# Routing spread over the output projection, and the last expert pair summed by TensorE, in a two-layer trunk with a mixture of experts

## The chip, the cores and the metric

One core of a Trainium2 chip runs the whole program. The metric is the device time of one execution in microseconds, the median over runs. All data is float32.

## What is computed

A trunk of two layers over 512 tokens of width 1024. Each layer is a token mixer (RWKV-7 in layer 0, stick-breaking attention in layer 1), a cross-attention into 256 memory rows, and a mixture of experts; each is normed before and added to `h`. The expert part of the reference, cut to what matters:

```python
g_logits = (t @ wg) + bg                       # 4 groups
group = jnp.argmax(g_logits, axis=-1)
p_group = jnp.take_along_axis(softmax(g_logits), group[:, None], axis=-1)
e_sel = ((t @ we) + be).reshape(-1, G, E)[group]   # 8 experts of that group
top_val, top_idx = lax.top_k(e_sel, 2)
top_w = softmax(top_val) * p_group
y = sum over the two experts: top_w * (silu(t @ w1) * (t @ w3)) @ w2
```

So each token goes to 2 of 32 experts. An expert has 3 MB of weights, 96 MB a layer.

## The kernel before

Every engine has its own instruction list, written out by hand, and they meet in semaphores (`S(name)`, `wait_ge`, `then_inc`). `h` lies in SBUF as four tiles of 128 tokens (`NT` = 4). Weights of the projections go through a ring of three 2 MB buffers (`ring`); the arena is shared out by address.

**The projection before the experts** (`cross_pe`, `project_tok`, L548). The output projection `xo` of the cross-attention runs in eight groups of eight matmuls: the four tiles for the left 512 columns, then for the right. DVE adds each to `h` (`add_to_h`, L578). In the right half PE turns the tile before (`late_turn`, L473, half way through a group), ACT and DVE copy the turned parts out (L483, L485), and after the group PE makes that tile's 36 scores (`route_logits`, L1661).

**Routing** (`moe_route_vec`, from L1704). When all four tiles have scores, DVE works out for all of them together: norm scale, best group, first and second expert, a running count (`chosen`). PE ranks the tokens within an expert with a triangular matrix (L1669, L1670). DVE then finds each token's slot, also those beyond 64 rows of an expert (overflow), makes 16 one-hot matrices, and PE sums products of them into a table of which token stands in which slot (L1674). The table is written at L1802. ACT scales the rows of `h` (L1682) and SP stores them to memory (`moe_rows_out`, L1829).

**The experts** (`moe_pe`). There are 16 pairs of experts, 64 rows each, n = 0 to 15. For each POOL gathers 128 rows (L1881), PE turns them (L1935), DVE copies them (L1940), PE multiplies up (L1950), ACT and DVE make the hidden row (L1955 to L1961), PE turns it (L1965) and multiplies down (L1975), ACT and DVE copy the result (L2041, L2061), POOL scatters it to memory (`ye_out`, L1906). PE's order is: up(n), turned hidden of n-1, turned rows of n+1, down(n-1). SP loads the weights (`moe_loads`, L1832, L1833 up, L1836 down). Pair 0's are loaded early, those of pair 1 (into the ring) after the projection, pair 2's up weights into a third buffer `w13x` once `h`'s rows are stored; everything later waits for `up_done` or `down_done` of an earlier pair.

**Overflow and combination.** `further` is a loop over overflow blocks; it reads their number from SBUF and here no block runs. Then POOL gathers for each tile the two rows of every token (`moe_combine_pool`, L1918), when all scatters have landed, and DVE adds both with their gates (`moe_combine_vec`, L1928). SP waits for these gathers, then loads the next layer's `sqkv` weights (L288). In layer 0 PE turns the tiles for the next mixer (L473) and starts its projection `sq` (L534); in layer 1 the final norm follows (`final_vec`, L418, L2179).

## Time and profile before

| what | us |
|---|---|
| median of 3 runs | 1868.31 (1867.97 to 1869.39) |
| the profiled execution | 1867.32 |
| its span | 1865.5 |
| busy PE, DVE, ACT, POOL | 1604.1, 581.8, 412.7, 167.6 |
| DMA moved | 313.84 MB |
| clock of PE over the span | 0.935 of 2.4 GHz |

Times in rows are microseconds from the start of the span. Busy shares mix stages with different limits, so the stages are to be read one by one; a window's row gives the busy time of each engine in it.

### The profile page before, as it was taken

How to read it: one execution, taken by the hardware profiler on the slowest of the kernel's cores; microseconds unless marked ns; L12 is line 12 of the kernel's file. 1: busy time of each engine (PE TensorE's matmuls, PEld its weight loads, DVE VectorE, ACT ScalarE, POOL GpSimd, SP SyncE). 2: the span in 40 equal slices, each digit the busy share in tenths (PEclk: the TensorE clock that was granted, in tenths of full speed). 3: DMA queues.
4: the chain of work that ended last, by engine and by line, in shares of the span. 5: the costliest groups of instructions: out<-in, count | busy, mean ns of one | idle time of the engine just before them, and what ended most of it. 6: DMA issues, size and time to landing. Idle time of an engine off the chain costs nothing.

```text
span 1865.5 us, 26366 instructions
## 1 busy us (share of the span) xinstructions
PE 1604.1 (86%) x11505; PEld 835.6 (45%) x11505; DVE 581.8 (31%) x1040; ACT 412.7 (22%) x805; POOL 167.6 (9%) x186
## 2 busy tenths in 40 slices
PE   4999989998899999669778589999999993988781
PEld 2444468886554454423233244446544542333330
DVE  5210766663651031332111221206310315121114
ACT  2103245553301221201000120017320312010001
POOL 2000123230000000011111200000000000111102
PEclk8999999999899999879899889999999996999896
DMA  6118000000541500279999541220033006799994
GB/s 227 45 58 297 0 3 4 4 4 28 207 150 45 225 1 4 112 295 417 425 423 425 227 172 72 90 77 14 1 136 135 4 0 280 288 423 425 425 397 160
DMA packets 82068, 313.84 MB, mean 168 GB/s; under 512 B 18088, under 2 KB 19168, under 8 KB 57184
## 3 DMA queue, kind: packets, MB, share of 16 engines
q1 hardware_dynamic: 70432, 286.95, 39.0%
q0 software_dynamic: 11520, 25.19, 3.6%
q8 instruction: 91, 1.49, 0.3%
q14 instruction: 25, 0.20, 0.0%
HBM read 305.81 MB, written 35.39 MB: 183 GB/s over the span
## 4 chain that ended last, share of the span: by engine, by line
PE 70%; issue 7%; DVE 5%; ACT 4%; DMA 2%; POOL 1%; POOLq 0%; DVEq 0%; SPq 0%; ACTq 0%; PEldq 0%
PE PS L548 16%; PE PS L1950 14%; PE PS L534 13%; PE PS L1002 7%; PE PS L1975 6%; PE PS L1326 2%; PE PS L1935 2%; PE PS L1302 1%; PE PS L1519 1%; PE PS L473 1%; PE PS L1540 1%; PE PS L1530 1%; DMA arena<-normed_rows,table 1%; PE PS L1135 1%; PE PS L1965 1%
## 5 line engine op out<-in xcount | busy, mean ns | idle before, releaser
L534 PE MATMUL PS<-arena,ring 128*128 128x512 f32 (+1 forms) x1024 | 416.2, 568 | 0.0
L548 PE MATMUL PS<-ring,arena 128*128 128x512 f32 x704 | 306.2, 593 | 0.7 <-ACT arena L1485 0.7
L534 PEld LDWEIGHTS PS<-arena,ring 128*128 128x128 f32 x1024 | 196.0, 192 | 216.7 <-issue 210.7
L548 PEld LDWEIGHTS PS<-ring,arena 128*128 128x128 f32 x704 | 132.5, 190 | 160.7 <-issue 159.8
L1950 PE MATMUL PS<-arena 128*64 128x512 f32 x512 | 134.9, 687 | 43.7 <-issue 41.0
L1950 PE MATMUL PS<-ring,arena 128*64 128x512 f32 x512 | 120.0, 623 | 26.4 <-issue 23.3
L1958 DVE TENSOR_TENSOR arena<-PS,arena 128x256 f32<-128x256 f32 x32 | 13.6, 425 | 314.8 <-PE PS L1965 295.5
L1950 PEld LDWEIGHTS PS<-arena 128*64 128x64 f32 x512 | 44.5, 158 | 132.5 <-issue 128.9
L562 ACT ACTIVATE arena<-PS 128x512 f32<-128x512 f32 (+1 forms) x56 | 31.7, 567 | 308.6 <-PE PS L534 308.6
L1955 ACT ACTIVATE arena<-PS 128x256 f32<-128x256 f32 x32 | 12.3, 384 | 375.6 <-PE PS L1950 375.6
L1950 PEld LDWEIGHTS PS<-ring,arena 128*64 128x64 f32 x512 | 42.4, 143 | 102.1 <-issue 98.6
L1002 PE MATMUL PS<-ring 64*64 64x64 f32 (+1 forms) x3072 | 74.8, 236 | 5.3 <-ACT ring L851 3.1
L1002 PEld LDWEIGHTS PS<-ring 64*64 64x64 f32 x3072 | 70.2, 135 | 13.8 <-issue 5.8
L578 DVE TENSOR_TENSOR h<-h,PS 128x512 f32<-128x512 f32 x32 | 22.0, 688 | 172.9 <-PE PS L548 172.9
L407 ACT ACTIVATE arena<-h 128x1024 f32<-128x1024 f32 x28 | 29.5, 1054 | 209.4 <-DVE h L578 172.3
L851 ACT ACTIVATE ring<-PS 128x512 f32<-128x512 f32 (+1 forms) x88 | 63.1, 753 | 53.0 <-PE PS L1002 48.9
L1881 POOL DMA_INDIRECT arena<-normed_rows,table x32 | 32.5, 1016 | 440.8 <-PE PS L1935 255.3
L1509 DVE TENSOR_TENSOR_SCAN arena<-arena 128x128 f32<-128x128 f32 (+3 forms) x64 | 48.2, 808 | 76.7 <-ACT arena L1471 76.7
L1893 POOL MEMSET arena<- 128x1024 f32 x4 | 3.7, 951 | 646.7 <-PE PS L548 646.7
L1975 PE MATMUL PS<-ring,arena 128*64 128x512 f32 x256 | 58.5, 598 | 1.0 <-issue 1.0
L1975 PE MATMUL PS<-arena 128*64 128x512 f32 x256 | 58.5, 598 | 1.0 <-issue 1.0
L473 PE MATMUL PS<-ident,h 128*128 128x128 f32 x160 | 32.9, 328 | 30.1 <-DVE h L1928 15.1
(274 smaller groups left out, 1797.8 us busy)
## 6 DMA issues: line engine op xcount, KB each, us to landing
arena<-in_moe_w SPq DMA_DIRECT2D x96, 1024.0 KB, 20.4
ring<-in_moe_w SPq DMA_DIRECT2D x96, 1024.0 KB
ring<-in_sb_wqkv SPq DMA_DIRECT2D x6, 2048.0 KB, 8.1
ring<-in_xa_wkv SPq DMA_DIRECT2D x4, 2048.0 KB, 15.5
ring<-in_xa_wq SPq DMA_DIRECT2D x4, 2048.0 KB, 8.1
ring<-in_xa_wo SPq DMA_DIRECT2D x4, 2048.0 KB, 13.6
h<-in_x SPq DMA_DIRECT2D x8, 512.0 KB, 5.3
ring<-in_rw_wr SPq DMA_DIRECT2D x2, 2048.0 KB, 13.3
```

The lines of the kernel that those rows point to most:

```text
L473: pe.transpose(PS[:, late_bank(name, n), 0:P], h[:, t, k::KC], ident[:, :]).then_inc(S("late_turned"), 1)
L534: ins = pe.matmul(PS[:, g % NBANK, 0:n], ring[:, u % RING, k, P * (j % 4):P * (j % 4) + P], xt[:, k, 0:n], start=(k == 0), stop=(k == KC - 1))
L548: ins = pe.matmul(PS[:, g % NBANK, :], xt[:, k, P * t:P * t + P], ring[:, (u0 + half) % RING, k, :], start=(k == 0), stop=(k == KC - 1))
L562: act.activation(dst[:, j, 0:n], group_out(act, g0 + j)[:, 0:n], ACT.Copy).then_inc(S("proj_out_A"), 1)
L851: act.activation(dst, src, ACT.Copy).then_inc(S("pair_act_out"), 1)
L1002: return pe.matmul(out, lhs, rhs, start=start, stop=True, skip_group_check=True)
L1326: ins = pe.matmul(PS[:, g % NBANK, :], memV[:, m, XD * x + P * v:XD * x + P * v + P], probT[x % 2][:, m, :], start=(m == 0), stop=(m == 1))
L1509: vec.tensor_tensor_scan(att[m][a][:, 0:nn][:, ::-1], fail[m][a][:, T - nn:T][:, ::-1], from_query[:, T - nn:T][:, ::-1], 1.0, ALU.mult, A ...
L1881: return pool.indirect_dma_start(out=xg[p][0:rows, :], out_offset=None, in_=scratch["rows"], in_offset=bass.IndirectOffsetOnAxis(ap=index, ...
L1935: ins = pe.transpose(bank(k // 4, 4, P)[:, k % 4, 0:rows], xg[p][0:rows, k::KC], ident[0:rows, 0:rows])
L1950: ins = pe.matmul(bank(2, 2, F)[r, :, :], xgT[p][:, k, r], w[a][:, :, k, :], start=(k == 0), stop=(k == KC - 1))
L1975: ins = pe.matmul(PS[r, 6 + half, :], hidT[:, k, r], w2e[p][a][:, k, 512 * half:512 * half + 512], start=(k == 0), stop=(k == 1))
```

## The change

1. `cross_pe` has its own loop. Turning of the tile before comes after the second matmul of a group, its scores after the fifth, and the rank products (`route_ranks`) of the tile before that after the seventh.
2. DVE works out each tile's routing between its additions to `h` (`moe_choice_vec`): `scale`, `group_and_first`, `second`, `place`. Only tile 3 is left at the end, with `second` of tile 2. The eight copies of tile 3's turned parts are all ACT's. ACT takes each tile's norm and issues the storing of its rows itself.
3. The table's one-hots know only the first 64 rows of an expert. The even expert of a pair is filled from the middle of its 128 slots downwards, the odd one upwards. Everything on overflow moves into DVE's work of pairs 0 to 3 (`over_counts`, `over_ranks`, `over_slots`, `over_rows`), with eight products on PE after up(4) (`over_table_pe`).
4. Pair 1's up weights are loaded during the projection (one expert after its first group, one after its fourth), in another layout of the ring. The last pairs' loads and PE work change order: down(14) before up(15).
5. Pair 15's rows are not stored. A matrix of gates (`spread_vec`, pair 5; turned by PE at pair 7, copied at pair 8) multiplies them on PE (`combine_last_pe`: eight matmuls 128x512, into PSUM), and DVE adds eight halves to `h` (`combine_last_vec`). The other rows are gathered as soon as pair 14's are stored, and DVE sums them (`combine_stored`) after pair 15's copy and before the branch of `further_vec`. Overflow rows are gathered and summed inside `further`.
6. SP no longer waits for the gathers before it loads `sqkv`; it waits for the last `down_done`. The first turned tile for layer 1 waits for two tiles of `h`.

The diff, cut to its core:

```diff
+            for half in range(2):
+                u = UNITS.index(xo) + half
+                unit_arrived(pe, u)
+                for t in range(NT):
+                    g = FIRST[xo] + NT * half + t
+                    bank_free(pe, g)
+                    for k in range(KC):
+                        if half == 0 and t == 0:
+                            group_evacuated(pe, FIRST[xv] + k)
+                        ins = pe.matmul(PS[:, g % NBANK, :], oT[:, k, P * t:P * t + P], ring[:, u % RING, k, :],
+                                        start=(k == 0), stop=(k == KC - 1))
+                        if half == 1 and t and k == 1:
+                            late_turn(pe, ffn, t - 1, h_tile_ready(xo))
+                        if half == 1 and t and k == 4:
+                            route_logits(pe, l, t - 1)
+                        if half == 1 and t >= 2 and k == 6:
+                            route_ranks(pe, l, t - 2)
+                    ins.then_inc(S("proj_filled"), 1)
+            late_turn(pe, ffn, NT - 1, h_tile_ready(xo))
+            route_ranks(pe, l, NT - 2)
+            route_logits(pe, l, NT - 1)
...
+            moe_choice_vec(vec, l)
...
-                late_turn(pe, "mix1", t, lambda e, t: e.wait_ge(S("h_moe0"), t + 1))
+                late_turn(pe, "mix1", t, lambda e, t: e.wait_ge(S("h_moe0"), min(t + 2, NT)))
...
+        w13 = [[split(arena[:, 6144 * a:6144 * a + 4096], [2, KC, F]) for a in range(2)],
+               [split(ringS[:, 4096 * (a + 1):4096 * (a + 2)], [2, KC, F]) for a in range(2)]]
+        w2e = [[split(arena[:, 6144 * a + 4096:6144 * a + 6144], [2, C]) for a in range(2)],
+               [split(ringS[:, 2048 * a:2048 * a + 2048], [2, C]) for a in range(2)]]
...
+        def route_ranks(pe, l, t):
+            pe.wait_ge(S("iota_ready"), 12)
+            pe.wait_ge(S("chosen"), 2 * (NT * l + t) + 1)
+            scores_read(pe, l, (2, 4, 5, 7)[t])
+            v = PS[:, 4, 256 + NE * t:256 + NE * t + NE]
+            pe.matmul(v, su[:, :], OOs[:, t, :], start=True, stop=False)
+            pe.matmul(v, ones[:, :], cum[:, t, :], start=False, stop=True).then_inc(S("ranked"), 1)
...
-            pe.wait_ge(S("chosen"), l + 1)
-            pe.wait_ge(S("iota_ready"), 9)
-            pe.matmul(PS[:, 4, 0:(NT + 1) * NE], su[:, :], OO.rearrange("p t e -> p (t e)"), start=True, stop=False)
-            pe.matmul(PS[:, 4, 0:(NT + 1) * NE], ones[:, :], cum.rearrange("p t e -> p (t e)"), start=False, stop=True)\
-                .then_inc(S("ranked"), 1)
-            for n in range(8):
-                pe.wait_ge(S("onehots"), 2 * (8 * l + n) + 2)
-                pe.matmul(PS[:, 5, 0:NCOL], OS[n % 2], OB[n % 2][:, 0:NCOL], start=(n == 0), stop=(n == 7))\
+            def filled_table(t):
+                pe.wait_ge(S("onehots"), 28 * l + 3 * (t + 1))
+                for k in range(2):
+                    ins = pe.matmul(PS[:, 5, 0:NPE], OS[:, t, k, :], OB[:, t, k, :], start=(t + k == 0),
+                                    stop=(t + k == NT))
+                return ins
+            for t in range(NT - 1):
+                filled_table(t)
+            route_ranks(pe, l, NT - 1)
+            filled_table(NT - 1).then_inc(S("tabled"), 1)
+            pe.wait_ge(S("chosen"), 2 * NT * (l + 1))
+            scores_read(pe, l, 8)
+            pe.matmul(PS[:, 4, 384:384 + NE], ones[:, :], cum[:, NT, :], start=True, stop=True).then_inc(S("ranked"), 1)
+        def over_table_pe(pe, l):
...
+                act.wait_ge(S("ffn_rstd"), 5 * l + (1, 2, 4, 5)[t])
+                act.activation(tnE[:, t, :], h[:, t, :], ACT.Copy, scale=rstd[:, t:t + 1]).then_inc(S("norm_rows"), 1)
+                act.wait_ge(S("norm_rows"), ROWS0[name] + t + 1)
+                act.dma_start(scratch["rows"][P * t:P * t + P, :], tnE[:, t, :]).then_inc(S("rows_out"), 16)
...
+            def second(t):
+                c = slice(t, t + 1)
+                O = O12[:, 1, t, :]
+                do(vec.scalar_tensor_tensor(out=mel2, in0=O12[:, 0, t, :], scalar=-2 * BIG, in1=mel, op0=ALU.mult,
+                                            op1=ALU.add))
+                first_equal(O, mel2, v2[:, c], s1[:, c], w32[:, :])
+                do(vec.tensor_scalar(O, O, s1[:, c], None, ALU.is_equal))
+                do(vec.tensor_tensor(mel2, O12[:, 0, t, :], O, ALU.add))
+                vec.tensor_tensor(OOs[:, t, :], mel2, sgn, ALU.mult).then_inc(S("chosen"), 1)
+                vec.wait_ge(S("chosen"), 2 * (NT * l + t) + 1)
+                vec.tensor_tensor(cum[:, t + 1, :], cum[:, t, :], OOs[:, t, :], ALU.add).then_inc(S("chosen"), 1)
+                o = O12[:, :, t, :].rearrange("p k (n a) -> p k n a", a=2)
+                vec.tensor_tensor(OB[:, t, :, :], o[:, :, :, 0], o[:, :, :, 1], ALU.add).then_inc(S("onehots"), 1)
...
+            def place(t):
+                vec.wait_ge(S("ranked"), (NT + 1) * l + t + 1)
+                rank = PS[:, 4, 256 + NE * t:256 + NE * t + NE]
+                vec.tensor_tensor(by_k, O12[:, :, t, :], rank.unsqueeze(1).to_broadcast([P, 2, NE]), ALU.mult)                    .then_inc(S("scores_read"), 1)
+                scores_read(vec, l, (3, 5, 6, 8)[t])
...
+            for t in range(NT - 1):
+                add(1, t)
+                late_evac(vec, f"ffn{l}", t, xTE, 1)
+                if t == NT - 2:
+                    place(0)
+                    vec.wait_ge(S("ffn_norm"), 9 * l + 7)
+                    vec.tensor_scalar(half_mean[:, :], half_sq[:, :], 1.0 / C, EPS, ALU.mult, ALU.add)\
+                        .then_inc(S("ffn_rstd"), 1)
+                scale(t)
+                group_and_first(t)
+                if t < NT - 2:
+                    second(t)
+            add(1, NT - 1)
+            second(NT - 2)
+            place(NT - 3)
+            place(NT - 2)
+            scale(NT - 1)
+            group_and_first(NT - 1)
+            second(NT - 1)
+            place(NT - 1)
...
+            assert UNITS.index(f"xo{l}") % RING == 2
+            load_up(sp, l, 2, w13[1][0], S("w13_in1"))
+            sp.wait_ge(S("proj_filled"), FIRST[f"xo{l}"] + 4)
+            load_up(sp, l, 3, w13[1][1], S("w13_in1"))
             sp.wait_ge(S("proj_filled"), FIRST[f"xo{l}"] + 8)
-            load_pair(sp, l, 1, 1)
+            for a in range(2):
+                load_down(sp, l, 2 + a, w2e[1][a], S("w2_in1"))
...
             for n in range(4, NPE):
-                if n + 1 < NPE:
+                if n + 1 < NPE - 1:
                     up_weights(n + 1)
                 down_weights(n)
+                if n + 1 == NPE - 1:
+                    up_weights(n + 1)
...
             for p in range(2):
-                pool.wait_ge(S(f"ye_out{p}"), 16 * (NPE // 2) * (l + 1))
-            pool.wait_ge(S("over_done"), l + 1)
...
+        def combine_stored(vec, l, t):
+            vec.wait_ge(S(f"yg_in{t}"), 32 * (l + 1))
+            for k in range(2):
+                m = NT * k + t
+                vec.scalar_tensor_tensor(out=h[:, t, :], in0=yg[2 * t + k], scalar=w_stored[:, m:m + 1], in1=h[:, t, :],
+                                         op0=ALU.mult, op1=ALU.add).then_inc(S("h_stored"), 1)
+                vec.wait_ge(S("h_stored"), 8 * l + 2 * t + k + 1)
+        def last_bank(t, half):
+            return (4 + 2 * t + half) % 8
+        def combine_last_pe(pe, l):
+            pe.wait_ge(S("gates_last"), 7 * l + 3)
+            pe.wait_ge(S("ye_a"), (NPE + 1) * (l + 1))
+            pe.wait_ge(S("ye_v"), (NPE + 1) * (l + 1))
             for t in range(NT):
-                vec.wait_ge(S(f"yg_in{t}"), 32 * (l + 1))
-                for k, w in enumerate((wA, wB)):
-                    if k:
-                        vec.wait_ge(S("h_half"), NT * l + t + 1)
-                    vec.scalar_tensor_tensor(out=h[:, t, :], in0=yg[2 * t + k], scalar=w[:, t:t + 1], in1=h[:, t, :],
-                                             op0=ALU.mult, op1=ALU.add)\
-                        .then_inc(S("h_half") if k == 0 else S(f"h_moe{l}"), 1)
+                for half in range(2):
+                    ins = pe.matmul(PS[:, last_bank(t, half), :], gatesT[:, t, :],
+                                    ye[1][:, 512 * half:512 * half + 512], start=True, stop=True)
+                ins.then_inc(S("gates_last"), 1)
+        def combine_last_vec(vec, l):
+            for t in range(NT):
+                vec.wait_ge(S("gates_last"), 7 * l + 4 + t)
+                for half in range(2):
+                    v = h[:, t, 512 * half:512 * half + 512]
+                    ins = vec.tensor_tensor(v, v, PS[:, last_bank(t, half), :], ALU.add)
+                ins.then_inc(S(f"h_moe{l}"), 1)
...
-                if n:
+                if n == 4:
+                    over_table_pe(pe, l)
+                if n == 7:
+                    spread_pe(pe, l)
+                if n and n < NPE - 1:
                     turn_hid_of(n - 1)
                 if n + 1 < NPE:
                     turn(n + 1)
-                if n:
+                if n and n < NPE - 1:
                     down_pair(n - 1)
-            turn_hid_of(NPE - 1)
-            down_pair(NPE - 1)
+                if n >= NPE - 2:
+                    turn_hid_of(n)
+                    down_pair(n)
...
-        def further(eng, l, body):
-            eng.wait_ge(S("over_known"), l + 1)
+                if n >= NPE - 2:
+                    rows(n)
+                if n < 4:
+                    (over_counts, over_ranks, over_slots, over_rows)[n](vec, l)
+                if n == 5:
+                    spread_vec(vec, l)
+                if n == 8:
+                    spread_out(vec, l)
+            for t in range(NT):
+                combine_stored(vec, l, t)
...
-            moe_rows_out(sp, 0)
             moe_loads(sp, 0)
             further_sp(sp, 0)
-            for t in range(NT):
-                sp.wait_ge(S(f"yg_in{t}"), 32)
             load_units(sp, at_unit("sqkv"), at_unit("xo1"))
...
                 moe_pool(pool, l)
+                moe_combine_pool(pool, l)
                 further_pool(pool, l)
-                moe_combine_pool(pool, l)
...
                 further_pe(pe, l)
+                combine_last_pe(pe, l)
...
-                moe_combine_vec(vec, l)
+                combine_last_vec(vec, l)
```

PE around the end of the output projection, before (L548 projection, L473 turning, L1661 scores, L1669 to L1674 ranks and table):

```order
L548 MATMUL PS<-ring,arena 128x512 x4
L473 MATMUL PS<-ident,h 128x128 x8
L548 MATMUL PS<-ring,arena 128x512 x4
L1661 MATMUL PS<-arena 128x36 x8
L473 MATMUL PS<-ident,h 128x128 x8
L1661 MATMUL PS<-arena 128x36 x8
L1669 MATMUL PS<-arena,masks 128x160
L1670 MATMUL PS<-arena,ones 128x160
L1674 MATMUL PS<-arena 128x31 x8
L1935 MATMUL PS<-ident,arena 128x128 x8
```

and after the change (L1351 projection, L484 turning, L1705 scores, L1722 and L1723 ranks, L1729 table):

```order
L1351 MATMUL PS<-ring,arena 128x512 x2
L1722 MATMUL PS<-arena,masks 128x32
L1723 MATMUL PS<-arena,ones 128x32
L1351 MATMUL PS<-ring,arena 128x512
L484 MATMUL PS<-ident,h 128x128 x8
L1722 MATMUL PS<-arena,masks 128x32
L1723 MATMUL PS<-arena,ones 128x32
L1705 MATMUL PS<-arena 128x36 x8
L1729 MATMUL PS<-arena 128x16 x6
L1722 MATMUL PS<-arena,masks 128x32
L1723 MATMUL PS<-arena,ones 128x32
L1729 MATMUL PS<-arena 128x16 x2
```

The scores of tile 2 have moved into the last group, and only tile 3's scores and ranks are left behind it, with six of the eight table products between them.

PE at the last pairs of layer 1, before (L1950 up, L1965 hidden turned, L1935 rows turned, L1975 down):

```order
L1950 MATMUL PS<-arena 64x512 x16
L1965 MATMUL PS<-ident,arena 128x128 x2
L1935 MATMUL PS<-ident,arena 128x128 x8
L1975 MATMUL PS<-ring,arena 64x512 x8
L1950 MATMUL PS<-ring,arena 64x512 x16
L1965 MATMUL PS<-ident,arena 128x128 x2
L1975 MATMUL PS<-arena 64x512 x8
L1965 MATMUL PS<-ident,arena 128x128 x2
L1975 MATMUL PS<-ring,arena 64x512 x8
L2081 TENSOR_LOAD over
```

and after (L2151 up, L2166 hidden turned, L2136 rows turned, L2176 down):

```order
L2151 MATMUL PS<-arena 64x512 x16
L2166 MATMUL PS<-ident,arena 128x128 x2
L2136 MATMUL PS<-ident,arena 128x128 x8
L2176 MATMUL PS<-ring,arena 64x512 x8
L2166 MATMUL PS<-ident,arena 128x128 x2
L2176 MATMUL PS<-arena 64x512 x8
L2151 MATMUL PS<-ring,arena 64x512 x16
L2166 MATMUL PS<-ident,arena 128x128 x2
L2176 MATMUL PS<-ring,arena 64x512 x8
L2301 TENSOR_LOAD over
```

Pair 14's down-projection has moved ahead of pair 15's up-projection, and the last turning and down follow it with nothing in between.

## Rows read from the trace of the kernel before

**Rows 1.** The page, part 2: DMA share in tenths, 40 slices.
```profile
DMA  6118000000541500279999541220033006799994
```

**Rows 2.** Windows, layer 0: span; busy us (count) by engine; PE clock; DMA share; GB/s.
```profile
771.00:804.10 33.10, 12.18 (x59) 10.72 (x58) 22.15 (x93) 9.56 (x16) 0.01 (x1) 0.55 0.74 300
...
824.10:1034.20 210.10, 178.53 (x820) 70.17 (x820) 39.94 (x73) 19.52 (x43) 26.31 (x26) 0.94 1.01 417
...
1054.90:1086.40 31.50, 8.29 (x32) 5.70 (x33) 14.92 (x23) 8.16 (x23) 8.57 (x9) 0.55 0.70 249
```

**Rows 3.** Timeline, second half of `xo0`: start, us, engine, line, operation, [idle before].
```profile
741.13 0.69 DVE L578 TENSOR_TENSOR h<-h,PS 128x512 f32<-128x512 f32 x1 [6.18 <-PE PS L548]
...
749.89 0.69 DVE L578 TENSOR_TENSOR h<-h,PS 128x512 f32<-128x512 f32 x1 [3.08 <-PE PS L548]
...
760.24 1.87 PE L1661 MATMUL PS<-arena 128*128 128x36 f32 x16
...
760.44 0.69 DVE L578 TENSOR_TENSOR h<-h,PS 128x512 f32<-128x512 f32 x1 [3.08 <-PE PS L548]
...
765.77 0.63 ACT L483 ACTIVATE arena<-PS,gainT 128x128 f32<-128x128 f32 x2 [3.46 <-PE PS L473]
...
770.98 0.69 DVE L578 TENSOR_TENSOR h<-h,PS 128x512 f32<-128x512 f32 x1 [3.08 <-PE PS L548]
```

**Rows 4.** Timeline, routing of layer 0 and its first gather.
```profile
774.50 3.46 PE L1661 MATMUL PS<-arena 128*128 128x36 f32 x16
...
778.10 0.31 DVE L1704 TENSOR_TENSOR arena<-PS,rstd 128x144 f32<-128x144 f32 x1 [1.47 <-PE PS L1661]
...
778.99 0.18 DVE L1709 TENSOR_TENSOR arena<-arena,masks 128x16 f32<-128x16 f32 x1
...
783.56 0.29 DVE L1728 TENSOR_TENSOR arena<-arena,masks 128x128 f32<-128x128 f32 x1
...
802.80 0.19 DVE L1802 TENSOR_SCALAR table<-PS 128x31 int32<-128x31 f32 x1 [0.73 <-PE PS L1674]
...
804.09 1.22 POOL L1881 DMA_INDIRECT arena<-normed_rows,table  x1 [88.56 <-PEq L2020]
...
811.78 1.97 PE L1935 MATMUL PS<-ident,arena 128*128 128x128 f32 x8 [9.02 <-DMA arena<-normed_rows,table]
```

**Rows 5.** Timeline, the first load behind pair 0, and pair 1's up.
```profile
824.10 0.33 SPq L1832 DMA_DIRECT2D arena<-in_moe_w  x1
...
826.66 7.09 PE L1950 MATMUL PS<-ring,arena 128*64 128x512 f32 x32 [1.52 <-DVE arena L1940]
```

**Rows 6.** Timeline of PE, the last pairs: down(13), up(15), down(15).
```profile
1030.51 3.65 PE L1975 MATMUL PS<-ring,arena 128*64 128x512 f32 x16
...
1036.18 8.79 PE L1950 MATMUL PS<-ring,arena 128*64 128x512 f32 x32 [2.02 <-issue]
...
1050.52 3.65 PE L1975 MATMUL PS<-ring,arena 128*64 128x512 f32 x16 [0.52 <-issue]
```

**Rows 7.** Timeline, the combination of layer 0.
```profile
1053.66 1.28 ACT L489 ACT_TABLE_LOAD   x1 [0.56 <-issue]
...
1055.76 0.97 POOL L1906 DMA_INDIRECT expert_rows<-arena,out_row  x1 [3.63 <-DVE arena L2061]
...
1060.34 0.98 POOL L1918 DMA_INDIRECT arena<-expert_rows,pos  x1 [3.61 <-SPq L2116]
...
1075.71 4.76 SPq L288 DMA_DIRECT2D ring<-in_sb_wqkv  x3
...
1078.16 0.61 DVE L485 TENSOR_SCALAR arena<-PS,gainT 128x128 f32<-128x128 f32 x2
```

**Rows 8.** Gathers L1881 (in the stream), then L1918 (after it): time to landing.
```profile
DMA to landing us min/median/max: 3.2/8.1/8.8
...
DMA to landing us min/median/max: 4.3/5.6/6.5
```

**Rows 9.** Timeline, the combination of layer 1.
```profile
1842.35 10.59 DVE L1928 SCALAR_TENSOR_TENSOR h<-arena,masks,h 128x1024 f32<-128x1024 f32 x8 [12.59 <-DMA arena<-expert_rows,pos]
```

More of the change, by code:

```diff
@@ L2135, in body @@
                 down(pe, 0, 1, 1).then_inc(st, 1)
+                step(at_step, 61)
             further(pe, l, body)
@@ L2163, in body, with sums @@
                 vec.tensor_copy(d, s).then_inc(st, 1)
-            further(vec, l, body)
+            def sums():
+                vec.wait_ge(S(f"over_rows_in{l}"), 8 * 16)
+                for m in range(8):
+                    t, k = m // 2, m % 2
+                    w = w_over[:, NT * k + t:NT * k + t + 1]
+                    vec.scalar_tensor_tensor(out=h[:, t, :], in0=yg[m], scalar=w, in1=h[:, t, :], op0=ALU.mult,
+                                             op1=ALU.add).then_inc(S(f"over_added{l}"), 1)
+                    vec.wait_ge(S(f"over_added{l}"), m + 1)
+            further(vec, l, body, sums)
         tnF = at(0, [NT, C])
```

399 lines of the change are left out of this document (242 added, 157 removed).

## The prediction

> **What bounds the kernel now.** I began with the page's DMA slices [rows 1]: two blocks of nines, the expert stages of the two layers, and little elsewhere. So I cut the first layer (the second runs the same code) into stretches [rows 2]. From 824.1 to 1034.2 the DMA share is 1.01 at 417 GB/s: 80 loads of 1 MB of expert weights and the pairs' token rows pass, while PE is busy 178.5 of 210.1: it has idle time there that it cannot use. This stream begins only when pair 0's up-projection has ended (SP issues at 824.10 [rows 5]), because every later load waits for a buffer. Nothing inside it can be shortened by PE or DVE; what counts is when it begins, and what follows its last bytes. Before it, from 771 to 804.1, PE does 12.2 us of work in 33 while DVE routes, then idles 9 for the first gather [rows 4]. After it, from 1054.9 to 1086.4, PE does 8.3 us in 31.5. In layer 1 DVE alone waits 12.6 and sums 10.6 there [rows 9]. These gaps are the change's ground.
>
> **1. The start of the stream.** Before, DVE begins routing all four tiles at once at 778.10, the table is written at 802.80, POOL issues the first gather at 804.09 and PE starts on it at 811.78 [rows 4]. One account serves for both layers.
> Now the tiles' routing lies inside the output projection. In its second half the h additions stand at 741.13, 749.89, 760.44 and 770.98 [rows 3]: 8.76 apart with the transposes alone in between, 10.54 with the logits too. After the change each of the three groups holds its transposes and logits: 741.13 + 3 x 10.54 = 772.75. Two things come on top. (a) DVE does 19 small steps (0.20 each, L1709's 0.18 in [rows 4] and the gap to its successor: 3.8) between the logits and the next h addition. The logits end 2.6 before the group does, and the next transposes come two matmuls (1.7) into the next group: with the addition's 0.7 it is ready 0.5 late, in two groups, 1.0. (b) Two rank products of some 0.4: 0.8. So the last addition starts at **774.5**, 3.5 later than before.
> From there: addition 0.7; tile 3 turned, all eight copies on ACT at 0.31 each (two take 0.63 in [rows 3]), 2.9, to 778.1; rank product of tile 2 and DVE's reading of it, on which the next logits wait, 1.0; last logits 3.46, as the row at 774.50 in [rows 4], at half clock (the stretch from 771 has a mean of 0.55, [rows 2]); then 17 dependent steps to `chosen` 3.5, to 786.1; the rank pair 1.2 (four passes at the logits' 0.22, and the handing over); four steps 1.0; two table products 0.9; table to POOL 1.3 (802.80 to 804.09). The sum is 790.5: the gather goes then instead of 804.1: **-13.6**. Its landing is taken as before (7.7 from issue to PE), since 4 MB of weights (w13x) still go out once the rows are stored, at about 784, and need 10 us. The stream then follows with the same 9 us for pair 0.
> Bounds: if a step is 0.33, as those over 128 columns were (L1728's 0.29 in [rows 4] and the gap), the 38 steps between additions and the 21 behind them cost 7.6 more: -6.0. If the clock holds at 2.4 GHz for the logits (1.87 in place of 3.46) and the gather lands in the 5.6 of [rows 8] instead of 7.7, it is -17.3. I take -13.6 since the new steps have 4 to 36 columns like those of 0.17 to 0.20.
>
> **2. Inside the stream.** About 22 us of DVE work per layer (overflow bookkeeping in pairs 0 to 3, spreading of the last gates in pairs 5 and 8) moves in here. DVE has 39.9 of work in 210.1 [rows 2], so over some 14 pairs 3 of work and 12 idle in each 15, and 4 to 5 us more in each of four pairs fits. The first pairs are shorter: up(1) starts at 826.66 and takes 7.1 [rows 5], with a down of 3.65 about 12 in all, still 9 idle. The one join is after pair 4's up-projection, where PE's eight overflow products alternate with DVE's one-hots: 3 us on PE, while some 6 to 8 us of loads are queued. The stream is not starved: **0**. Bounds: 0 to +5 per layer. One pair's scatter less is left out.
>
> **3. The last pairs.** Pair 14's down-projection moves ahead of pair 15's up [rows 6]. Pair 13's down ends at 1034.2, PE then idles 2.0 and up(15) runs 8.79 at partly half clock. Now turn and down(14) fill this gap: 1034.2 + 1.3 + 3.65 = 1039.1; up(15) at full clock 7.1 as up(1) in [rows 5], 1046.2; sigmoid, two products, turning and copy, now uncovered, 2.7; down(15) 3.65: 1052.5 against 1054.2, **-1.7**. Its weights were in by 1036.18; pair 14's 2 MB now go ahead of them, 5.0 at 417 GB/s, so by 1041.2 at the latest, 2.1 after PE would want them. Bounds: with that and 8.79 for up(15), +2.1; below, -1.7 itself.
>
> **4. The combination.** Before, the scatter at 1055.76 has to land before the first gather at 1060.34; DVE ends its eight sums only at 1078.2 [rows 7]. Now pair 14's scatter goes at 1040.8, lands 4.6 later, and the eight gathers issue from 1045.4 at 1.25 each; the last at 1054.2. DVE still takes its eight stored sums only after pair 15's copy, in its program order: 1053.3 + 6 x 1.32 ([rows 9]: 10.59 for eight) = 1061.2. The last gather would be in at 1059.8 (5.6 landing). But SP now issues 6 MB of `sqkv` at 1052.5, which it did at 1075.7 before; gathers inside a busy stream land in 8.1 [rows 8], so 1062.3: a wait of 1.1. Two sums, 1064.9; DVE's branch on the overflow count 0.6 (ACT's, ahead of its table load, is 0.56 in [rows 7]); then eight additions from PSUM of 0.69, as in [rows 3]: 1071.0. PE's eight products with the gates (8 at 0.86, as the two matmuls' 1.7 above: 6.9) end at 1061 under this. The turning and copying of four tiles needed 8.2 after DVE was free (1078.16 to the end of the last stretch of rows 2): 1079.2 against 1086.4, **-7.2** with the -1.7 inside.
> The Trainium skill, "DMA: Bandwidth & Descriptors", section "Queues, rings and completion order", says that each DMA engine takes turns, packet by packet, between the queues that have work. By it the four gathers still out at 1052.5 would run at half pace, be in at 1064.8 instead of 1062.3, and the sum would be 2.5 higher; the trace shows busy gathers only with the 8.1 of rows 8, which is what my sum uses.
> In layer 1 no weights follow [rows 9]: DVE's last copy ended at 1842.35 - 12.59 = 1829.76, now 1828.1; eight sums 10.6; branch 0.6; additions 5.5: 1844.8 against 1852.94, **-8.1**; the final norm behind it is unchanged, 12.6.
>
> **Sum.** 2 x 13.6 + 7.2 + 8.1 = 42.5. The profiled execution took 1867.3, 1.0 below the median of 1868.3: 1867.3 - 42.5 + 1.0 = 1825.8, so **1826**.
>
> **Rivals.** (A) The projection is held up more than I count, because DVE's chain (reciprocal, logits, 19 steps) stands ahead of the h addition that PE's transposes need. For: by my count the addition is already 0.5 late, so every further us is PE's. Against: the steps are short. With 0.33 a step: 1826 + 15 = 1841; half of that is as likely, 1833. (B) The stream gives something back: its first pairs are paced by PE (about 12 us each), the queue is only just full, and a late pair leaves the DMA engines empty. 5 per layer: 1836. (C) Better: the start wins 17.3 per layer, and PE, which no longer idles 15 us, is at full clock when it turns the tiles: 1826 - 7.4 - 3 = 1816. (D) Slower: the work taken from before the table comes back in full in the pairs. Price: 22 us a layer, plus 3 for the join at pair 4, so 50: 1876. It decides if DVE's idle time per pair is less than the inserted 4 to 5 us; by part 2 it is 9 to 12. (E) The change does not do what it says, if the gathers are issued early but all wait for pair 15 (a semaphore count or POOL's order): then the start remains, and each tail has the old wait, 1.7 less, and 6.1 of branch and additions more: 1826 + 15.3 + 2 x 4.4 = 1850, still faster.
>
> **How the numbers follow.** Forecast 0.60 (its own range 1819 to 1833), A 0.14, B 0.07, C 0.11, E 0.02, D 0.03, and 0.03 for a mixture that ends near no change. For eight times in ten I take the forecast, most of C and A: 1814 to 1840. About 0.2% is what a measurement of this kernel can tell from no change. Faster 0.94, same 0.02, slower 0.04.
>
> **What would show it.** The step at 1: the first gather on POOL 13 to 14 earlier relative to the projection's first group, the table write near +48 after 741; the h additions 10.5 to 11.5 apart. At 2: DMA share still 1.0 from pair 0's up to the end, the stretch still 210 long. At 3 and 4: down(14) before up(15), DVE's eight sums directly after the last copy with at most one wait, eight additions behind, and `sq` starting 25 to 27 after the last down-projection. I am wrong if the stretch of the stream is longer by more than 5, if the h additions lie over 12.5 apart, or if DVE waits for gathers at its first sums.

## The result, and the profile after

The changed kernel takes **1840.91 us** (median of 4 runs, 1839.65 to 1844.42) against 1868.14 of the kernel before (4 runs, 1865.76 to 1869.39): ratio **0.9859**, 95% interval 0.9842 to 0.9876. It is faster, by 27 us. The forecast was 1826, 42.5 us, and the range ended at 1840: the direction held, the time lies just outside.

The profiled execution has a span of 1838.9 (before 1865.5). I cut both into six intervals: **g**, start to the first gather on POOL; **a**, from there to the end of down(15) in layer 0; **b**, to the first matmul of `sq`; **c**, to the first gather of layer 1; **d**, to the end of its down(15); **e**, to the end. Each number is a difference of two timeline rows, in us. The experiments of the next section stand in the same table; before and after were each profiled twice.

| kernel | g | a | b | c | d | e | span |
|---|---|---|---|---|---|---|---|
| before | 804.1 | 250.1 | 32.4 | 491.0 | 251.4 | 36.5 | 1865.5 |
| before again (e10) | 804.9 | 249.5 | 32.1 | 493.7 | 252.7 | 36.9 | 1869.8 |
| after | 792.9 | 254.2 | 28.8 | 478.6 | 254.9 | 29.5 | 1838.9 |
| after again (e5) | 793.4 | 254.9 | 25.5 | 480.9 | 253.6 | 29.4 | 1837.8 |
| e1 routing only | 790.7 | 252.8 | 43.0 | 478.7 | 250.0 | 37.2 | 1852.5 |
| e2 up loads first | 791.2 | 257.7 | 26.3 | 483.6 | 258.7 | 29.5 | 1847.1 |
| e3 last pairs as before | 791.0 | 250.5 | 39.0 | 478.8 | 249.9 | 37.5 | 1846.6 |
| e4 sqkv held | 795.1 | 250.8 | 26.4 | 480.9 | 253.8 | 29.4 | 1836.3 |
| e6 routing only, sqkv held | 791.4 | 250.7 | 32.7 | 478.6 | 247.0 | 37.1 | 1837.4 |
| e7 last four by products | 787.7 | 252.6 | 25.9 | 479.0 | 249.5 | 29.8 | 1824.5 |
| e8 the same, sqkv held | 792.6 | 250.2 | 25.9 | 479.0 | 249.4 | 29.8 | 1826.8 |
| e9 down(14)'s load cut | 788.7 | 248.8 | 28.8 | 480.8 | 247.0 | 32.7 | 1827.0 |

The page's DMA slices, to [rows 1]: the same two blocks of nines.

```profile
DMA  6119000000532411269999832211015024799994
```

Windows of the changed kernel for the routing's end, the stream, the last pairs and the combination, layer 0 (columns as in [rows 2]):

```profile
779.00:793.00 14.00, 9.50 (x50) 8.50 (x49) 8.95 (x46) 6.50 (x17) 0.07 (x1) 0.66 0.82 307
815.10:1026.00 210.90, 181.27 (x841) 72.49 (x842) 58.24 (x147) 19.51 (x43) 26.49 (x26) 0.94 1.01 417
1026.00:1047.10 21.10, 15.30 (x68) 5.71 (x68) 2.23 (x4) 3.13 (x6) 6.70 (x7) 1.00 0.63 227
1047.10:1075.90 28.80, 15.43 (x49) 8.86 (x50) 20.70 (x32) 9.01 (x24) 3.29 (x3) 0.72 0.85 316
```

The stretch between the last addition and the gather has shrunk from 33.1 to 14.9 (the window leaves out its first 0.9). The stream still has 1.01 of the DMA at 417 GB/s, and in 210.90 VectorE now works 58.24 where it worked 39.94 in 210.10 [rows 2]: the moved 18 us cost at most 0.8 there. The start, on the timeline of DVE and POOL:

```profile
743.63 0.69 DVE L1801 TENSOR_TENSOR h<-h,PS 128x512 f32<-128x512 f32 x1 [6.16 <-PE PS L1351]
755.93 0.68 DVE L1801 TENSOR_TENSOR h<-h,PS 128x512 f32<-128x512 f32 x1
767.60 0.68 DVE L1801 TENSOR_TENSOR h<-h,PS 128x512 f32<-128x512 f32 x1
778.05 0.69 DVE L1801 TENSOR_TENSOR h<-h,PS 128x512 f32<-128x512 f32 x1 [0.71 <-PE PS L1351]
791.66 0.18 DVE L1881 TENSOR_SCALAR table<-PS 128x16 int32<-128x16 f32 x1 [1.13 <-PE PS L1729]
...
792.93 1.23 POOL L2040 DMA_INDIRECT arena<-normed_rows,table  x1 [74.97 <-PEq L2225]
```

The two middle additions have no idle time before them: DVE comes to them straight from routing. They lie 12.3 and 11.7 apart, 10.5 at the last, and the gather follows the first addition by 49.3, against 63.0 in [rows 3, 4].

Now the end, PE's timeline in layer 1 (L2176 down, L2166 hidden turned, L2151 up; the rows answer to [rows 6]):

```profile
1778.30 3.65 PE L2176 MATMUL PS<-ring,arena 128*64 128x512 f32 x16
1781.88 0.51 PE L2166 MATMUL PS<-ident,arena 128*128 128x128 f32 x2
1782.91 3.65 PE L2176 MATMUL PS<-arena 128*64 128x512 f32 x16 [0.52 <-issue]
1792.23 9.52 PE L2151 MATMUL PS<-ring,arena 128*64 128x512 f32 x32 [5.66 <-issue]
1803.14 0.50 PE L2166 MATMUL PS<-ident,arena 128*128 128x128 f32 x2 [1.39 <-issue]
1804.16 5.24 PE L2176 MATMUL PS<-ring,arena 128*64 128x512 f32 x16 [0.52 <-issue]
```

down(14) follows down(13) at once, as meant. But then PE stands 5.66 before up(15), runs it in 9.52, where 7.09 is full clock [rows 5], and down(15) in 5.24 instead of 3.65. The granted clock of 1782.00 to 1809.40 is 0.81. From the end of down(13) to that of down(15) it takes 27.5, in layer 0 21.1 (a wait of 3.35); before it was 20.2 and 20.0. During the wait the DMA is full:

```profile
1786.60:1792.20 5.60, 0.00 (x0) 0.00 (x0) 0.69 (x1) 0.00 (x0) 0.98 (x1) 0.83 1.00 411
```

The combination on DVE, layer 0 (L2086 stored sums, L2109 additions of the products), which answers to [rows 7] and [rows 9]:

```profile
1047.73 2.60 DVE L2086 SCALAR_TENSOR_TENSOR h<-arena,h 128x1024 f32<-128x1024 f32 x2
1050.54 2.60 DVE L2086 SCALAR_TENSOR_TENSOR h<-arena,h 128x1024 f32<-128x1024 f32 x2 [0.21 <-issue]
1053.98 2.61 DVE L2086 SCALAR_TENSOR_TENSOR h<-arena,h 128x1024 f32<-128x1024 f32 x2 [0.84 <-DMA arena<-expert_rows,pos]
1058.89 2.60 DVE L2086 SCALAR_TENSOR_TENSOR h<-arena,h 128x1024 f32<-128x1024 f32 x2 [2.30 <-DMA arena<-expert_rows,pos]
1062.65 4.87 DVE L2109 TENSOR_TENSOR h<-h,PS 128x512 f32<-128x512 f32 x8 [1.16 <-issue]
```

No wait before the first sum, 0.84 and 2.30 for late gathers, 4.87 for the eight additions.

### The profile page after: what moved, and what is told of

Same layout as the page of the kernel before. It is cut to its first block, busy times and chain, and to the rows that moved or that the text cites. A ratio compares the mean times of both kernels' runs of the same rounds, so it can differ in the third digit from the quotient of the medians.

```text
span 1838.9 us, 26793 instructions
## 1 busy us (share of the span) xinstructions
PE 1629.1 (89%) x11605; PEld 849.3 (46%) x11605; DVE 622.0 (34%) x1214; ACT 416.8 (23%) x823; POOL 166.1 (9%) x187
## 4 chain that ended last, share of the span: by engine, by line
PE 71%; issue 7%; DVE 5%; ACT 3%; DMA 2%; POOL 1%; DVEq 0%; PEld 0%; POOLq 0%; ACTq 0%
PE PS L545 14%; PE PS L2151 13%; PE PS L559 10%; PE PS L1013 7%; PE PS L2176 6%; PE PS L1351 5%; PE PS L1337 2%; PE PS L2136 2%; PE PS L1313 1%; PE PS L484 1%; PE PS L1548 1%; PE PS L1569 1%; PE PS L1559 1%; PE PS L1146 1%; PE PS L1705 1%
## 5 line engine op out<-in xcount | busy, mean ns | idle before, releaser
L2151 PE MATMUL PS<-ring,arena 128*64 128x512 f32 x512 | 126.8, 652 | 42.7 <-issue 39.7
L2151 PE MATMUL PS<-arena 128*64 128x512 f32 x512 | 127.1, 654 | 27.1 <-issue 24.3
L1351 PE MATMUL PS<-ring,arena 128*128 128x512 f32 x256 | 113.6, 595 | 0.0
L2159 DVE TENSOR_TENSOR arena<-PS,arena 128x256 f32<-128x256 f32 x32 | 13.6, 425 | 267.3 <-PE PS L2166 222.0
L2151 PEld LDWEIGHTS PS<-ring,arena 128*64 128x64 f32 x512 | 42.5, 150 | 124.9 <-issue 121.5
L2156 ACT ACTIVATE arena<-PS 128x256 f32<-128x256 f32 x32 | 12.3, 384 | 371.7 <-PE PS L2151 371.7
L2151 PEld LDWEIGHTS PS<-arena 128*64 128x64 f32 x512 | 43.0, 151 | 109.5 <-issue 105.9
L1351 PEld LDWEIGHTS PS<-ring,arena 128*128 128x128 f32 x256 | 47.5, 191 | 53.6 <-issue 53.6
L2176 PE MATMUL PS<-ring,arena 128*64 128x512 f32 x256 | 60.0, 612 | 1.0 <-issue 1.0
L2176 PE MATMUL PS<-arena 128*64 128x512 f32 x256 | 58.5, 598 | 1.0 <-issue 1.0
L494 ACT ACTIVATE arena<-PS,gainT 128x128 f32<-128x128 f32 x88 | 28.4, 365 | 135.1 <-PE PS L484 134.7
```

The source lines that it names most:

```text
L1351: ins = pe.matmul(PS[:, g % NBANK, :], oT[:, k, P * t:P * t + P], ring[:, u % RING, k, :], start=(k == 0), stop=(k == KC - 1))
L2151: ins = pe.matmul(bank(2, 2, F)[r, :, :], xgT[p][:, k, r], w[a][:, :, k, :], start=(k == 0), stop=(k == KC - 1))
L2176: ins = pe.matmul(PS[r, 6 + half, :], hidT[:, k, r], w2e[p][a][:, k, 512 * half:512 * half + 512], start=(k == 0), stop=(k == 1))
```

## The experiments

The theory after this reading: **(T1)** the routing's early start is nearly the whole gain; **(T2)** the products and the new order of the last pairs cancel, because the DMA is full up to the last weights, and what is moved ahead in the queue makes up(15) late. Rivals: the order of SP's issues alone costs (one could mend it); the products are worth their forecast and the loss lies elsewhere.

### e1 and e6: the early routing alone

```diff
-            do(vec.tensor_scalar(is_last, e8, float(NE - 2), None, ALU.is_ge))
+            do(vec.tensor_scalar(is_last, e8, float(NE + 2), None, ALU.is_ge))
...
-            for n in range(NPE - 1):
+            for n in range(NPE):
...
-            return NPE // 2 - p
+            return NPE // 2
...
-                combine_last_pe(pe, l)
...
-                combine_last_vec(vec, l)
```

with the last pairs' order of before on all engines, and each token block announced after its sums. e6 also has the old hold:

```diff
+            for t in range(NT):
+                sp.wait_ge(S(f"yg_in{t}"), 32)
             load_units(sp, at_unit("sqkv"), at_unit("xo1"))
```

> The early routing alone: the last two experts' rows are stored and gathered like all others, the last pairs run in the order of before (their loads too), and the sums by products, their spreading of the gates and the additions are left out; the state of the routing is as in the changed kernel, and the sums of a token block are announced before the rows beyond an expert's block could be added, which this data never has. Theory M, read from the two traces: the products and the new order of the last pairs together bring next to nothing (layer 0: end of the last down product to sq 28.8 against 32.4 us, but stream start to that end 2.0 longer; layer 1: 16.9 against 23.9, but 7.3 longer), so nearly the whole measured gain is the routing's: 1842 us (1839 to 1846), 0.986 of before. Rival N, the prediction's own terms: the products are worth 8.9 us in layer 0 and 9.8 in layer 1, so without them the kernel stands at 1841 + 19 = 1860 us.

> The early routing alone, and the loads of sqkv wait for layer 0's eight gathers as before the change. In the run of the routing alone those loads went out at the end of down(15) and the gathers and sums of layer 0 took until 33.3 us after it, against 24.1 in before, and down(15) to sq took 42.98 us against 32.40. Theory K (contention: 4 MB of gathered rows and the loads share the DMA): down(15) to sq comes back to 32 to 33 us, the first projection of layer 1 ends perhaps 2 us later, and the whole comes out 8 to 10 us below the routing alone, at 0.987 to 0.988 of before. Rival L (the long tail came from something else in that execution): within 2 us of it, 0.992.

Measured: e1 1855.32 us, 0.9924 (0.991 to 0.9937) of the kernel before. That lies between M and N, and interval b says why: 43.0. Its sums (DVE, layer 0) wait for gathers every time:

```profile
1062.49 2.60 DVE L2084 SCALAR_TENSOR_TENSOR h<-arena,h 128x1024 f32<-128x1024 f32 x2 [18.18 <-DMA arena<-expert_rows,pos]
1066.47 2.61 DVE L2084 SCALAR_TENSOR_TENSOR h<-arena,h 128x1024 f32<-128x1024 f32 x2 [1.39 <-DMA arena<-expert_rows,pos]
1070.46 2.60 DVE L2084 SCALAR_TENSOR_TENSOR h<-arena,h 128x1024 f32<-128x1024 f32 x2 [1.38 <-DMA arena<-expert_rows,pos]
1074.23 2.60 DVE L2084 SCALAR_TENSOR_TENSOR h<-arena,h 128x1024 f32<-128x1024 f32 x2 [1.16 <-DMA arena<-expert_rows,pos]
```

and with the hold (e6) two rows are left:

```profile
1053.67 2.60 DVE L2084 SCALAR_TENSOR_TENSOR h<-arena,h 128x1024 f32<-128x1024 f32 x2 [10.90 <-DMA arena<-expert_rows,pos]
1056.89 8.11 DVE L2084 SCALAR_TENSOR_TENSOR h<-arena,h 128x1024 f32<-128x1024 f32 x6 [0.61 <-DMA arena<-expert_rows,pos]
```

The combine gathers of layer 0 took, first in e1, then in e6:

```profile
DMA to landing us min/median/max: 7.4/9.9/12.3
```
```profile
DMA to landing us min/median/max: 4.2/5.9/6.2
```

The gathers wait in turn for the last store, which the loads hold up as well. First gather and what it waited for, POOL, e1 and then e6:

```profile
1053.10 0.98 POOL L2074 DMA_INDIRECT arena<-expert_rows,pos  x1 [6.97 <-DMA expert_rows<-arena,out_row]
```
```profile
1047.12 0.98 POOL L2074 DMA_INDIRECT arena<-expert_rows,pos  x1 [2.52 <-DMA expert_rows<-arena,out_row]
```

e6 came to 1843.12 us, 0.987 (0.9846 to 0.9895), with b back at 32.7. K holds: loads beside the last store and the gathers cost about 10 us when that store comes late. And beside it, on the same chip, stands **e5**, the changed kernel again: 1839.65 us, 0.9861 (0.9835 to 0.9888).

> The changed kernel once more, so that the others of this call stand beside it on one chip. If its interval against before (0.984 to 0.988) holds, it comes out at 0.986 of before.

The routing alone gives 25 us; products, reordering and the earlier loads of `sqkv` together add 3.5, inside the intervals. T1 holds. "The routing alone" is parts 1 to 3 of the change with the early loads of pair 1 and the gathers and sums ahead of `further`; these were not timed one by one. Against e6 the changed kernel (mean of two profiles) gains 5.5 in b and 7.6 in e and loses 3.9 in a and 7.3 in d: that is the cancelling of T2 in numbers.

### e2: the loads' order of before

```diff
-                if n + 1 < NPE - 1:
+                if n + 1 < NPE:
                     up_weights(n + 1)
                 down_weights(n)
-                if n + 1 == NPE - 1:
-                    up_weights(n + 1)
```

> The changed kernel, but SP issues the loads of pair 15's up weights ahead of pair 14's down weights, as before the change; TensorE's order stays the changed one. Theory O (the order of the issues costs): up(15) finds its weights there and doesn't wait (3.35 us in layer 0, 5.66 in layer 1, and half clock in layer 1), while down(14) finds its own too: 1841 - 9 - 2 = 1830 us. Rival F (the DMA is full to about us 1036, share 1.01 to 1.03 in nearly every stretch of 5 us before it): whatever comes first, 4.2 MB of up weights are 10 us of the stream, so down(14) is then late by about what up(15) gains: it starts 2 to 4 us later in each layer, with its store and the gathers behind it, and the time is 1843 us (1840 to 1848). I hold F likelier.

1848.8 us, 0.9872 (0.985 to 0.9894): no gain. As this interval overlaps that of the changed kernel, a loss is to be read from a and d alone. PE's timeline in layer 1:

```profile
1783.08 3.65 PE L2174 MATMUL PS<-ring,arena 128*64 128x512 f32 x16
1786.66 0.51 PE L2164 MATMUL PS<-ident,arena 128*128 128x128 f32 x2
1796.61 6.35 PE L2174 MATMUL PS<-arena 128*64 128x512 f32 x16 [9.44 <-DMA arena<-in_moe_w]
1802.80 7.03 PE L2149 MATMUL PS<-ring,arena 128*64 128x512 f32 x32
```

up(15) no longer waits; down(14) does, 9.44, and everything stands behind it. a and d grow by about 3 and 4.5. O falls. F was right in kind and too small in size: I counted 2 to 4 for a wait that became 9.44 (8.49 in layer 0), of which the vanished wait of up(15) gives back 5.66.

### e3: the products, with the last pairs' order of before

The edit of e2, and `if n` in place of `if n and n < NPE - 1` on PE, ACT and DVE, pair 15's steps last.

> The changed kernel with its products, but the last pairs on TensorE, ScalarE, VectorE and SP in the order of before: up(15), then turn and down of pair 14, then those of pair 15. Theory R (reordering lost more than it gave): down(15) ends 4 us earlier in layer 0 and 7 in layer 1, and as the products wait for it the end comes that much earlier: 1830 us. Rival G (the gathers of the stored rows set the end of the sums): down(14) ends some 8 us later than now, its store and the eight gathers with it, and the sums on VectorE end 4 to 8 us later than now in each layer: 1853 us (1848 to 1858). I hold G likelier, which would say that the reordering pays although it makes up(15) wait.

1848.39 us, 0.989 (0.9874 to 0.9906). R falls, G holds: a is 250.5 and d 249.9, some 4 shorter than with the reordering, but b is 39.0 and e 37.5. In e it equals e1 to 0.3 us: **in layer 1 the products bring nothing with the order of before**, since the stored rows still come last. In layer 0, where both run without the hold, b is 4.0 shorter than in e1, and as a whole e3 is 0.3% below it (0.989 against 0.9924). In b the row of the first sum waits 9.37 after the last copy:

```profile
1051.56 2.61 DVE L2084 SCALAR_TENSOR_TENSOR h<-arena,h 128x1024 f32<-128x1024 f32 x2 [9.37 <-DMA arena<-expert_rows,pos]
```

The reordering is thus needed for the products to pay in layer 1 (8 us in e), and costs 4 of them again in d. For layer 0 that is not shown: e3 was not run with the hold, and the 32.7 of e6 shows what the hold can do in b.

### e4: sqkv held until the gathers landed

The three lines that e6 adds, in the changed kernel.

> The changed kernel, but SP issues the loads of the next layer's first projection weights (sqkv) only when the eight combine gathers of layer 0 have landed, as before the change. Theory Q (those loads slow the gathers: 8.3 to 8.7 us to landing in layer 0 against 6.0 to 6.3 in layer 1, where nothing is loaded beside them): the gathers land in about 6.2 us, the waits of the sums (0.84 and 2.30 us) go, sums end 3 us earlier, 1838 us. Rival W: the weights are then issued about 8 us later, and as they took 12.7 to 22.3 us to land, the first projection waits for the later ones: 1841 to 1846 us. I expect 1841 (1837 to 1846).

1839.72 us, 0.983 (0.9814 to 0.9846), against 0.9861 of e5 on another chip. The intervals overlap; b is 26.4, between the 28.8 and 25.5 of the two executions of the changed kernel. The gathers landed after 6.1 in the median, as Q said, but in e5 they did so without the hold (5.9). Whether the hold is worth anything here stays open: the ratios differ by 0.3%, b by at most 2.4. It doesn't bring the 10 us that it is worth against e1, since here the gathers go out before the loads.

### e9: fewer bytes ahead of up(15)

```diff
+                    if n == NPE - 2:
+                        sp.dma_start(w2e[0][a][0:8], experts(A["moe_w2"], l, 2)[2 * n + a][0:8]).then_inc(S("w2_in0"), 16)
+                        continue
                     load_down(sp, l, 2 * n + a, w2e[n % 2][a], S(f"w2_in{n % 2}"))
```

> The changed kernel, but of pair 14's down weights only 8 of 128 partitions are loaded (its product then takes pair 12's weights in the other 120, so the output is not the reference's): 1.97 MB less in each layer, 4.7 us of the stream at 417 GB/s, and nothing else is changed, no instruction and no wait. Theory D (the stream of weights fills the DMA, so the 2.1 MB that now stand ahead of up(15)'s 4.2 MB are what up(15) waits for): the weights of up(15) land 4 to 5 us earlier, its wait (3.35 and 5.66 us) all but goes in layer 1 too, and the time from the first gather to the end of down(15), 254 us in each layer, falls by 3.5 to 5: 8 to 9 us over both layers, 1832 us. Rival S (SP's waits hold the issue back, not the bytes): the issues stand at the same places, up(15) waits as before, within 2 us of the changed kernel.

1829.18 us, 0.9805 (0.9783 to 0.9828). PE in layer 1:

```profile
1773.07 3.65 PE L2179 MATMUL PS<-ring,arena 128*64 128x512 f32 x16
1776.65 0.51 PE L2169 MATMUL PS<-ident,arena 128*128 128x128 f32 x2
1777.68 3.65 PE L2179 MATMUL PS<-arena 128*64 128x512 f32 x16 [0.52 <-issue]
1781.13 7.07 PE L2154 MATMUL PS<-ring,arena 128*64 128x512 f32 x32
1789.59 0.50 PE L2169 MATMUL PS<-ident,arena 128*128 128x128 f32 x2 [1.39 <-DVE arena L2165]
1790.61 3.65 PE L2179 MATMUL PS<-ring,arena 128*64 128x512 f32 x16 [0.52 <-issue]
```

No instruction was moved, 1.97 MB a layer were taken out, and up(15) starts as down(14) ends and takes the 7.07 of full clock. a and d fall by 5.7 and 7.2 against the mean of the changed kernel's two executions. Of that, up(15)'s start, counted from the layer's first gather, gives 5.2 and 4.1, near the 4.7 of the bytes. The other 0.5 and 3.1 lie behind its start, where up(15) took 9.2 to 9.8 in three of the four cases of the changed kernel. D holds, S falls; T2 is shown, together with e2. In e 3 us come back, since the gathers now end after PE.

### e10: before, once more

> The kernel before, once more with a profile: how far the intervals that are compared (first gather to the end of down(15), that end to sq, sq to layer 1's first gather) repeat when nothing is changed. I expect each within 2 us of 250.1, 32.4 and 491.0, and the first gather, which sums all that lies before it, within 3 us of 804.1.

Its six intervals lie within 3 of the first ones; c misses my bound of 2 by 0.7. So single intervals are good to about 3 us; g moves by up to 7.4 between kernels that are equal up to there (787.7 to 795.1 in ten profiles, mean 791.5).

### e7 and e8: a version that beats both

If no stored row has to wait for pair 14 either, the order of before can stay, and the gathers go out under the last pairs. So both last pairs are summed by products:

```diff
+            do(vec.tensor_scalar(is_14, e8, float(NE - 4), None, ALU.is_ge))
...
-            for n in range(NPE - 1):
+            for n in range(NPE - 2):
...
+            for t in (0, 2):
+                product(t, gatesT14, 0, True, False)
+            pe.wait_ge(S("ye_a"), (NPE + 1) * (l + 1))
+            pe.wait_ge(S("ye_v"), (NPE + 1) * (l + 1))
+            for t in range(NT):
+                if t % 2:
+                    product(t, gatesT14, 0, True, False)
+                product(t, gatesT, 1, False, True).then_inc(S("gates_last"), 1)
```

with pair 14's gates spread in pairs 9 to 12, the edit of e3, and overflow rows kept in `xg[1]`. e8 adds the hold.

> A version for the wait that the reordering brought: pairs 14 and 15 (the last four experts) are both summed by TensorE products, 16 of 1.06 us or less at 128x512 (0.89 each in the changed kernel), accumulated in the same banks, and the last pairs and their loads go in the order of before, since no stored row waits for pair 14 now. The last store is pair 13's, some 20 us before the end of down(15). Theory P: stream to down(15) as short as with the order of before (gather to down(15) end 250.5 in layer 0, 250.0 in layer 1, against 254.2 and 254.9 in the changed kernel), and from down(15) to the last addition about 17 us (16 products 14.2, copies and the last addition 3) against 20.4 in layer 0 and 16.9 in layer 1: some 8 us faster than the changed kernel, 0.981 to 0.983. Rival H: the gathers (4 MB) are now issued while the last weights are loaded, both share the DMA, and up(15), down(14) or down(15) wait: 3 to 8 us longer in each layer, which takes it all back: 0.985 to 0.989.

> The version of the last four experts, and the loads of sqkv wait for layer 0's eight gathers. As these are issued about 10 us earlier than in the changed kernel, they have landed or nearly when down(15) ends, so the hold costs the next projection little. Theory: within 3 us of the same version without the hold, to the better side if the gathers of tokens 256 to 511 still waited for the loads there. Rival: sqkv arrive later and the first projection of layer 1 waits: 2 to 4 us slower.

e7: **1827.25 us** (1826.28 to 1832.21), 0.9793 (0.9769 to 0.9817), against 0.9861 of the changed kernel on the same chip: 12 us faster than that and 41 faster than before. e8: 1829.43, 0.9802 (0.978 to 0.9824), the same. Layer 0 of e7, PE, DVE and POOL:

```profile
1021.27 9.85 PE L2160 MATMUL PS<-ring,arena 128*64 128x512 f32 x32 [3.45 <-issue]
...
1036.69 3.65 PE L2185 MATMUL PS<-ring,arena 128*64 128x512 f32 x16 [0.52 <-issue]
1040.27 14.00 PE L2100 MATMUL PS<-arena 128*128 128x512 f32 x32
```
```profile
1040.99 10.52 DVE L2089 SCALAR_TENSOR_TENSOR h<-arena,h 128x1024 f32<-128x1024 f32 x8
1053.03 4.87 DVE L2120 TENSOR_TENSOR h<-h,PS 128x512 f32<-128x512 f32 x8 [1.52 <-issue]
```
```profile
1019.41 0.98 POOL L2068 DMA_INDIRECT expert_rows<-arena,out_row  x1 [11.52 <-DVE arena L2286]
1029.27 0.98 POOL L2079 DMA_INDIRECT arena<-expert_rows,pos  x1 [8.88 <-DMA expert_rows<-arena,out_row]
```

The last store goes at 1019.41, 21 us before down(15) ends, and the eight sums run without a wait under the products. b and e keep the changed kernel's values, a and d are 1.9 and 4.8 shorter; e8, with g at 792.6, is 11.0 shorter than the changed kernel's mean over a to e. Theory P holds in kind, and gave too little (0.981 to 0.983). Against that mean e7's span is 13.9 shorter, of which 8.4 lie in a to e and 5.4 in g, where the kernels are alike. H does not come: the gathers beside the last weights cost at most 2 in a (252.6 against the 250.5 of e3).

## Why the prediction was right and wrong

| interval | predicted | measured (means of two profiles each) |
|---|---|---|
| g | -13.6 | -11.3 (ten profiles with the early routing: -13.0) |
| a | -1.7 | **+4.8** |
| b | -5.5 | -5.1 |
| c | -13.6 | -12.6 |
| d | -1.7 | **+2.2** |
| e | -6.4 | -7.2 |
| sum | -42.5 | -29.3 |

**Part 1 held.** The gather stands 49.3 after the first addition; 790.5 less 741.13 [rows 3] was 49.4. That g shows only -11.3 lies ahead of it: the first addition itself stands 2.3 later in these two profiles than in the two of before, and in the ten it lies anywhere from 738.2 to 745.8. Inside, two sizes were off and cancelled: the last addition follows the first by 34.4, where I had 33.4 (DVE's chain stands in front of two additions, rival A's mechanism at a price of 1), and what follows the last addition took 14.9 instead of 16.0. PE started on the first gather after 8.9, not 7.7, in this profile, after 7.5 in layer 0 of the second, and after 5.9 and 6.5 in layer 1.

**Part 2 held.** 0 was taken, and 210.9 against 210.1 measured. Rival D did not come: DVE's idle time covered it. a as a whole grew, on the mean of two profiles, behind the stream. (Of the 4.1 of the profile shown, 2.1 lie ahead of it: the first load behind pair 0 goes out 22.1 after the gather, before 20.0, in e5 19.6.)

**Part 3 failed**, and with it the forecast. From the end of down(13) to that of down(15) the two executions of before took 20.0 and 17.3 in layer 0, 20.2 and 22.9 in layer 1; those of the changed kernel 21.1 and 26.8, 27.5 and 25.5: +5.3 and +5.0 in place of -1.7 each, 13.7 us off, of which the stream before it gave back 0.6 and 2.8. I put the forecast at "-1.7" and "+2.1" as the bound, by taking up(15)'s weights "by 1041.2 at the latest, 2.1 after PE would want them" and then leaving that wait out of the sum. What was measured lies even beyond that bound. The rows said which it was: the DMA share is 1.01 to the end of the stream [rows 2], so 2 MB moved ahead must make the 4 MB behind them 5.0 late. Counted from the layer's first gather, up(15) starts 6.5 later than before in layer 0 and 4.5 in layer 1, and without the 2 MB (e9) both are back to within 1.4. Besides, the wait may take the clock: up(15) 9.52 and down(15) 5.24 in layer 1, 4.0 more. I had given up(15) "full clock", since the gap before it was to be filled; the gap is longer than the 2.0 of [rows 6]. e4, the third profile with this order, has 250.8 and 253.8 in a and d. Over the three, the order costs 4.9 in d against the five kernels with early routing and the order of before (mean 249.2, no overlap), but only 1.9 in a (251.4), where the two groups overlap. None of the three signs by which I would have known myself wrong looks at this wait, and none of them came.

**Part 4 held in its sum**, b -5.1 and e -7.2 against -5.5 and -6.4, though not in its pieces, and b is the mean of -3.5 and -6.7. Pair 14's scatter landed 8.8 after its issue in layer 0 and 9.4 in layer 1 (4.6 [rows 7] predicted), while the last weights still pass; the gathers were hidden all the same as down(15) ended later too. The late gathers: my 8.1 [rows 8] stood for those beside `sqkv`; the trace has, for all eight of layer 0,

```profile
DMA to landing us min/median/max: 8.3/8.5/8.7
```

and DVE waited 0.84 and 2.30, 3.1 in place of 1.1. The second profile (e5) has 5.9 in the median there and no wait:

```profile
1048.97 10.52 DVE L2086 SCALAR_TENSOR_TENSOR h<-arena,h 128x1024 f32<-128x1024 f32 x8
```

So that the sum of this part came out is in part luck. The Trainium skill's "DMA: Bandwidth & Descriptors", "Queues, rings and completion order" (queues with work take turns), would have had the last gather in 2.5 later than my sum. Here my row was the better guide (8.5 against 8.1, where that rule gives 10.6). In e1, where all eight gathers ran beside the loads, they took 9.9 in the median and up to 12.3, against 5.9 and 6.2 with the hold: the slowest took twice as long, as at half pace, the median 1.7 times.

The other rivals: B's place was wrong, the first pairs lost nothing, though its price (5 a layer) is near what part 3 lost; A's price came out at 1 of its 15; C did not come, since the start's gain was as forecast and no more; E did not occur.

## What to carry to other kernels

Where a stretch is bound by the DMA, the order of loads decides only who waits: moving bytes ahead delays what stands behind them by size over rate, and this must be a term of the sum, not a bound. Work that is moved under such a stretch is free as long as its engine has idle time there; so take the long step (store, gather) out of the tail by making its last input earlier than the stream's end, as e7 does, instead of hurrying that input through the stream. When a change has several parts, time one without the others, but with its old waits: e1 without the old hold misled by 10 us.

## What the runs showed that I had not expected

- A wait for weights can cost more than itself. The 32 matmuls of up(15) took 7.07 after none (e9) and 7.09 after 3.35 (changed kernel, layer 0, granted clock 1.00), but 9.85 after 3.45 (e7), 9.78 after 4.63 (e5) and 9.52 after 5.66; in e2, after 9.44, down(14) took 6.35 instead of 3.65. The length of the wait alone does not decide it: after 2.02 the kernel before took 8.79 [rows 6], after 2.05 e6 took 7.09 in layer 1. What does, the runs don't show.
- A store of 128 rows issued while weights still pass needs 8.8 to 10.4 until the gathers may start (e7, layer 0: 1019.41 to 1029.27); behind the stream 3.5 (e6) to 5.1, 4.6 in [rows 7], and 7.9 beside the loads of `sqkv` (e1).
- Removing a wait of SP can cost 10 us: in e1 the next weights met the last store and the gathers that everything waited for.
